# Third attention layer: score products in three single-pass parts instead of one four-pass float32 product

## Chip, cores and metric

One core of one Trainium2 chip runs the whole program. The metric is the device time of one launch in microseconds (us), the median of several runs; lower is better.

## What is computed

Three transformer layers over 512 tokens of width 1024, all in float32: an mLSTM layer (A), a chunked attention layer with relative positions (B), and a third layer (C), each followed by a gated feed-forward part. Only layer C is touched. Cut to what matters:

```python
# differential attention: 4 heads, each with two maps (c = 0, 1) of 64 dimensions
s = einsum('bqhcd,bkhcd->bhcqk', q, k) * d ** -0.5 - slopes * dist
p = softmax(s); a = p[:, :, 0] - lam * p[:, :, 1]; o = a @ v
# neighbourhood attention: 8 heads of 64 dimensions, on a grid 64 wide
s = einsum('bqhd,bikhd->bhqik', q, k) * d ** -0.5 + bias     # a mask of -1e30 outside 16 columns
o = softmax(s) @ v
```

## The kernel before

**Number formats.** Weights and activations of the large products are split into a high part, rounded to the format `F32R`, and a low part, the float32 value less the high one. One large product is then three products of `F32R` parts (helper `three`, L1410 to L1412: high times low, low times high, high times high), each of which TensorE does in one pass. Products on plain float32 tiles are issued as one `matmul`, which the trace shows as two MATMUL records.

**Layer C's attention** is written out by hand for each engine, in a function `attention_c` of its own for ScalarE (L807), VectorE (L1249) and TensorE (L1620), over `C_STEPS` = 32 steps and a few to drain. A step is one tile of 128 queries (`qt`, 0 to 3) of one pair of maps or heads (`n`, 0 to 7): steps 0 to 15 are the four differential heads with their two maps, steps 16 to 31 four pairs of neighbourhood heads. So a pair takes four steps, and a pair changes between steps 3 and 4, 7 and 8, and so on, seven times. In a step `s`

- TensorE makes the scores (L1639): for `a` = 0 and 1 one float32 product of 64 rows (partitions 0 to 63, or 64 to 127) by 128 queries by 512 keys, out of `qk` (queries and keys of the differential heads) or `qkb` (of the neighbourhood heads), into PSUM banks 4 and 5. It then does, in a third each, the "units" of a background stream (`units_of`: the projections of layer C still to come, three `F32R` products of L1410 to L1412 for each k-tile), and between them the transposes of the probabilities of step `s` - 1 (L1670). In the second step of a pair it multiplies the previous pair's probabilities with the values (L1647, L1652), in the third a norm's sum (L1658, differential heads only).
- VectorE takes each score row set out of PSUM with its bias and minimum (L1284), shrinks the slope tile `absd` at the end of a pair (L1288), finishes a head (`yaw`, L1291, in the last step of a pair), evacuates a block of the stream that has ended (`epilogue_of`, L963 or L968), makes the low part of a block of weights (`split_of`, L915), and last turns the exponentials into probabilities (L1311 to L1323).
- ScalarE does the two exponentials (L825), casts (L836, L851), copies the transposes out of PSUM (L844), and makes the high part of the weights (L566).

Each engine takes its instructions strictly in the order written; semaphores connect the engines. `s_done` says that scores are made, `s_biased` that they are out of PSUM, `w_lo` that a block of weights is split.

**The neighbourhood bias** `rpt` (two slots; with 224 KB for a pair of heads in four loads, L412) is loaded from a DRAM scratch by SyncE's queue, among the loads of weights (`load_c_stream`); GpSimd adds the mask to each slot as it lands (L553). Slots 0 and 1 are both loaded at the end of layer B.

**Before step 0** VectorE turns two sums into norm factors in a chain (`both_norms`): reciprocal, two products (L1233, L1235), a copy (L1236), one `split_of` (L915), reciprocal (L1239), product (L1241), on which TensorE waits with the transposes of L1745.

## Time and profile before

| | |
|---|---|
| runs | 2100.31 to 2101.47 us, median 2100.87 us (3 runs) |
| the profiled execution's own time | 2098.9 us |
| its span, first to last instruction | 2097.2 us |
| TensorE busy | 2020.0 us of the span (96%) |
| VectorE, ScalarE, GpSimd busy | 1072.9, 732.7, 37.7 us |
| mean granted TensorE clock | 0.988 of full |
| attention of layer C, step 0 to the last score | 1320.3 to 1546 us of the span |

Times of a row count from the first instruction. A busy time is the union of records, so two products that run side by side count once. "Idle before" is how long an engine stood still ahead of an instruction, with the instruction that released it.

### The profile page before, as it was taken

Reading aid. Unit: us, or ns where it says so; the run is one execution under the profiler, and the core shown is the slowest. Engines: PE = TensorE matmul, PEld = TensorE weight load, DVE = VectorE, ACT = ScalarE, POOL = GpSimd, SP = SyncE. Lnnn points to the kernel's source line nnn. Section 1 sums busy time; section 2 is a strip of 40 time slices with the busy share of each in tenths; the row PEclk is TensorE's granted clock in tenths of the full one; section 3 lists DMA queues with packets and bytes.
Section 4 is the critical chain, followed back from the end, with each engine's and each line's share of the span. In section 5 each row is a group of like instructions: output and inputs, shape, how many; then the busy total and the mean of one; then the engine's idle time right before and its main releaser. Section 6 shows DMA issues by size and latency. Waiting matters only on the chain.

```text
span 2097.2 us, 24349 instructions
## 1 busy us (share of the span) xinstructions
PE 2020.0 (96%) x9435; PEld 1596.2 (76%) x9435; DVE 1072.9 (51%) x1432; ACT 732.7 (35%) x1030; POOL 37.7 (2%) x64
## 2 busy tenths in 40 slices
PE   7999989999999999989999998999999969999998
PEld 5867768888888777668888887766768848888887
DVE  4444565534555444465534557666545565543544
ACT  4444442222233344342222233344433333222222
POOL 1000000000000000000000001000000000000000
PEclk9999999999999999999999999999999989999999
DMA  3211133333324322033333335113222313333322
GB/s 126 81 60 51 41 92 104 86 109 101 93 75 133 101 81 66 31 105 100 85 100 97 92 88 136 60 61 78 58 81 81 100 40 100 95 90 95 100 80 80
DMA packets 297974, 180.15 MB, mean 86 GB/s; under 512 B 22295, under 2 KB 294784, under 8 KB 297896
## 3 DMA queue, kind: packets, MB, share of 16 engines
q1 hardware_dynamic: 297880, 179.08, 29.8%
q8 instruction: 51, 0.84, 0.2%
q14 instruction: 27, 0.22, 0.0%
q10 hardware_dynamic: 16, 0.02, 0.0%
HBM read 176.85 MB, written 2.20 MB: 85 GB/s over the span
## 4 chain that ended last, share of the span: by engine, by line
PE 89%; DVE 6%; ACT 3%; issue 2%; SPq 0%; DMA 0%; DVEq 0%; ACTq 0%
PE psum L1410 27%; PE psum L1412 26%; PE psum L1411 26%; PE psum L1639 2%; DVE wl L915 1%; PE psum L1592 1%; PE psum L1670 1%; PE psum L1601 1%; PE psum L1566 1%; PE psum L1563 1%; PE psum L1614 1%; PE psum L1647 1%; PE psum L1652 1%; ACT wh L566 1%; DVE ss L924 1%
## 5 line engine op out<-in xcount | busy, mean ns | idle before, releaser
L915 DVE TENSOR_TENSOR wl<-stage,wh 128x2048 fp32r<-128x2048 f32 (+3 forms) x182 | 367.6, 2020 | 125.3 <-ACT wh L566 124.5
L566 ACT CAST wh<-stage 128x2048 fp32r<-128x2048 f32 (+3 forms) x182 | 307.1, 1688 | 214.0 <-PE psum L1412 207.4
L1410 PE MATMUL psum<-xl,wh 128*128 128x512 f32 x800 | 327.5, 409 | 11.5 <-DVE xl L930 9.3
L1410 PE MATMUL psum<-x2l,wh 128*128 128x512 f32 x768 | 304.6, 397 | 12.0 <-DVE wl L915 12.0
L1412 PE MATMUL psum<-xh,wh 128*128 128x512 f32 x800 | 313.7, 392 | 0.0
L1411 PE MATMUL psum<-xh,wl 128*128 128x512 f32 x800 | 313.3, 392 | 0.0
L1411 PE MATMUL psum<-x2h,wl 128*128 128x512 f32 x768 | 300.8, 392 | 0.0
L1412 PE MATMUL psum<-x2h,wh 128*128 128x512 f32 x768 | 300.6, 391 | 0.0
L1410 PE MATMUL psum<-hidl,wh 128*128 128x512 f32 x528 | 205.8, 390 | 2.6 <-DVE wl L915 2.6
L1410 PEld LDWEIGHTS psum<-xl,wh 128*128 128x128 f32 x800 | 151.2, 189 | 72.6 <-issue 35.6
L1411 PE MATMUL psum<-hidh,wl 128*128 128x512 f32 x528 | 205.4, 389 | 0.0
L1412 PE MATMUL psum<-hidh,wh 128*128 128x512 f32 x528 | 205.4, 389 | 0.0
L604 ACT ACTIVATE work<-work 128x512 f32<-128x512 f32 x66 | 41.7, 632 | 408.7 <-DVE work L991 408.7
L1410 PEld LDWEIGHTS psum<-x2l,wh 128*128 128x128 f32 x768 | 145.4, 189 | 45.0 <-DVE wl L915 10.1
L1412 PEld LDWEIGHTS psum<-xh,wh 128*128 128x128 f32 x800 | 151.0, 189 | 32.5
L1411 PEld LDWEIGHTS psum<-xh,wl 128*128 128x128 f32 x800 | 151.5, 189 | 30.7 <-issue 2.6
L1412 PEld LDWEIGHTS psum<-x2h,wh 128*128 128x128 f32 x768 | 145.3, 189 | 30.6
L1411 PEld LDWEIGHTS psum<-x2h,wl 128*128 128x128 f32 x768 | 145.4, 189 | 30.3 <-issue 0.7
L991 DVE TENSOR_TENSOR work<-psum,rs 128x512 f32<-128x512 f32 x66 | 45.4, 688 | 211.1 <-PE psum L1412 211.1
L1410 PEld LDWEIGHTS psum<-hidl,wh 128*128 128x128 f32 x528 | 99.1, 188 | 24.2 <-DVE wl L915 3.8
L1410 PE MATMUL psum<-wl,xh 128*128 128x256 f32 x384 | 115.4, 301 | 1.6 <-DVE qk L963 0.8
L1412 PEld LDWEIGHTS psum<-hidh,wh 128*128 128x128 f32 x528 | 99.1, 188 | 20.8
(270 smaller groups left out, 2579.4 us busy)
## 6 DMA issues: line engine op xcount, KB each, us to landing
stage<-in_ffn_w_gate_dram SPq DMA_DIRECT2D x44, 512.0 KB, 4.0
stage<-in_ffn_w_up_dram SPq DMA_DIRECT2D x44, 512.0 KB, 5.3
stage<-in_w_in_dram SPq DMA_DIRECT2D x40, 512.0 KB, 4.0
stage<-in_a_w_in_dram SPq DMA_DIRECT2D x24, 512.0 KB, 4.8
stage<-in_ffn_w_down_dram SPq DMA_DIRECT2D x32, 384.0 KB, 3.8
stage<-in_w_gate_dram SPq DMA_DIRECT2D x22, 512.0 KB, 4.0
stage<-in_w_up_dram SPq DMA_DIRECT2D x22, 512.0 KB, 5.2
stage<-in_ffn_w_down_dram SPq DMA_DIRECT2D x32, 320.0 KB, 3.8
```

Of the source, the lines that this page charges most:

```text
L566: nc.scalar.copy(wh[:, par, 0:n], stage[:, par, 0:n]).then_inc(w_hi, 1)
L604: nc.scalar.activation(work[:, 1, :], work[:, 0, :], ACT.Sigmoid).then_inc(h_sig, 1)
L915: vec.tensor_tensor(wl[:, par, 0:n], stage[:, par, 0:n], wh[:, par, 0:n].bitcast(F32), ALU.subtract).then_inc(w_lo, 1)
L924: vec.tensor_tensor(ss[:, :], ss[:, :], work[:, buf, :], ALU.add).then_inc(ss_added, 1)
L991: vec.tensor_tensor(work[:, 0, :], ps[:, 0, :], rs[:, :], ALU.mult).then_inc(h_in, 1)
L1410: mm(out, a_hi, b_lo, start=start, stop=False)
L1411: mm(out, a_lo, b_hi, start=False, stop=False)
L1412: return mm(out, a_hi, b_hi, start=False, stop=stop)
L1563: mm(psum[:, 6 - 2 * a, t * P:S], av[:, 2 * p + a, t, :], pt[:, a, t, 0:S - t * P], start=(t == 0), stop=(t == TT - 1))
L1566: last = mm(psum[:, 7 - 2 * a, t * P:S], ones[:, :], pt[:, a, t, 0:S - t * P], start=(t == 0), stop=(t == TT - 1))
L1592: mm(psum[:, 4 + a, 0:n], bq[rows, p % 4, qt * P:(qt + 1) * P], bk[rows, p, 0:n], start=True, stop=True).then_inc(s_done, 1)
L1639: mm(psum[:, 4 + a, :], t[rows, n % 4, qt * P:(qt + 1) * P], t[rows, 4 + n % 4, :], start=True, stop=True).then_inc(s_done, 1)
```

## The change

Two tiles are new: `qka` (at 79 KB of the region; it lies over slot 1 of `rpt`) for the differential heads, and `qkn` (at 8 KB, over the keys in `qk`) for the neighbourhood heads. Each holds four tiles of 128 by 512: query high, key high, query low, key low, of one pair at a time. ScalarE makes the two high parts of the next pair (`heads_hi`) in the last step of a pair, after the scores of that step (`s_done`) and after its copies, ahead of its weight cast. VectorE makes the two low parts (`heads_lo`), one as each high part arrives, in the same step after its epilogue and weight split and ahead of the reciprocal. TensorE waits for both low parts (`c_lo`) ahead of the first scores of a pair, and makes three products where it made one, alternating between the two row halves. Slot 1 of `rpt` is first loaded after step 15 instead of before layer C.

```diff
+        qka = at("qka", 79, [P, 4, S], F32R)
+        qkn = at("qkn", 8, [P, 4, S], F32R)
...
             def load_neighbour_bias(p):
 
-                if p < 2:
+                if p == 0:
                     sp.wait_ge(mm_done, st["down11"].b0)
                 else:
                     sp.wait_ge(s_biased, C_SCORE0 + 2 * (DA_STEPS + 4 * (p - 1)))
...
                 load_neighbour_bias(0)
-                load_neighbour_bias(1)
-                p = 2
+                p = 1
...
+            def heads_hi(n):
+
+                t, d = (qk, qka) if n < DA_HEADS else (qkb, qkn)
+                act.wait_ge(block_out, st["C_k" + ("a0", "a1", "b0", "b1")[n // 2]].b0 + 1)
+                if n:
+                    act.wait_ge(s_done, C_SCORE0 + 8 * n)
+                if n == DA_HEADS:
+                    act.wait_ge(c_lo, 2 * DA_HEADS)
+                nc.scalar.copy(d[:, 0, :], t[:, n % 4, :]).then_inc(c_hi, 1)
+                nc.scalar.copy(d[:, 1, :], t[:, 4 + n % 4, :]).then_inc(c_hi, 1)
...
+                    if part == 3 and s + 1 < C_STEPS:
+                        heads_hi(n + 1)
                     for b in c_stream.splits(s):
                         split_of(b)
...
+            def heads_lo(n):
+                t, d = (qk, qka) if n < DA_HEADS else (qkb, qkn)
+                for i in range(2):
+                    dve.wait_ge(c_hi, 2 * n + i + 1)
+                    vec.tensor_tensor(d[:, 2 + i, :], t[:, 4 * i + n % 4, :], d[:, i, :].bitcast(F32),
+                                      ALU.subtract).then_inc(c_lo, 1)
...
                     for b in c_stream.splits(s - 1):
                         split_of(b)
+                    if qt == TT - 1 and s + 1 < C_STEPS:
+                        heads_lo(n + 1)
...
-                        if qt == 0 and n % 2 == 0:
-                            pe.wait_ge(block_out, st["C_k" + ("a0", "a1", "b0", "b1")[n // 2]].b0 + 1)
+                        if qt == 0:
+                            pe.wait_ge(c_lo, 2 * (n + 1))
                         if s:
                             pe.wait_ge(s_biased, C_SCORE0 + 2 * s)
-                        t = qk if s < DA_STEPS else qkb
-                        for a in range(2):
-                            rows = slice(DH * a, DH * a + DH)
-                            mm(psum[:, 4 + a, :], t[rows, n % 4, qt * P:(qt + 1) * P], t[rows, 4 + n % 4, :],
-                               start=True, stop=True).then_inc(s_done, 1)
+                        d = qka if s < DA_STEPS else qkn
+                        for part, (i, j) in enumerate(((0, 3), (2, 1), (0, 1))):
+                            for a in range(2):
+                                rows = slice(DH * a, DH * a + DH)
+                                last = mm(psum[:, 4 + a, :], d[rows, i, qt * P:(qt + 1) * P], d[rows, j, :],
+                                          start=(part == 0), stop=(part == 2))
+                                if part == 2:
+                                    last.then_inc(s_done, 1)
```

The first pair's parts are made ahead of step 0 (`heads_hi(0)` after the table load L816, `heads_lo(0)` ahead of the work on `absd`).

VectorE's queue in step 7, the last of the second pair, before (L1284 scores out of PSUM, L1288 `absd`, L1291 `yaw`, L1311 to L1319 the probabilities):

```order
L1284 ISA work,rowmax<-psum,absd 128x512 [waits t_done,s_done]
L1284 ISA rowmax 128x1
L1288 TENSOR_SCALAR absd<-absd 128x896 [waits s_biased]
L1291 SCALAR_TENSOR_TENSOR yaw<-psum,gains,ss 128x512 [waits d_rs]
L1311 RECIPROCAL rowinv<-rowsum 128x2 [waits s_exp]
```

and as changed (line numbers of the changed kernel):

```order
L1308 ISA work,rowmax<-psum,absd 128x512 [waits t_done,s_done]
L1308 ISA rowmax 128x1
L1312 TENSOR_SCALAR absd<-absd 128x896 [waits s_biased]
L1315 SCALAR_TENSOR_TENSOR yaw<-psum,gains,ss 128x512 [waits d_rs]
L1269 TENSOR_TENSOR qka<-qk,qka 128x512 [waits c_hi] x2
L1337 RECIPROCAL rowinv<-rowsum 128x2 [waits s_exp]
```

Two subtractions, each with a wait for ScalarE, have come in ahead of the reciprocal; in steps 3, 11, 19 and 27 an epilogue and a weight split stand between the scores and these two.

ScalarE's queue in the same step, as changed (L839 exponentials, L850 the cast of `yah`, L858 the copy of the transposes, L568 the weight cast):

```order
L839 ACTIVATE work,rowsum<-work,rowmax 128x512 [waits s_biased] x2
L850 CAST yah<-yaw 128x512 [waits d_full]
L858 COPY pt<-psum 128x4x128 [waits t_done]
L817 CAST qka<-qk 128x512 [waits s_done,block_out]
L818 CAST qka<-qk 128x512
L568 CAST wh<-stage 128x2048 [waits mm_done,w_loaded1]
```

The two casts of L817 and L818 are new, between the copy and the weight cast.

SyncE's queue at the end of layer B, where the bias loads stand among those of the weights, before

```order
L412 DMA rpt<-rp_scratch 64x14x64 [waits mm_done]
L412 DMA rpt<-rp_scratch 64x14x64 x3
L412 DMA rpt<-rp_scratch 64x14x64 [waits mm_done]
L412 DMA rpt<-rp_scratch 64x14x64 x3
L400 DMA stage<-in_w_in_dram 128x4x256 [waits w_lo]
```

and as changed

```order
L403 DMA stage<-in_w_in_dram 128x4x256
L415 DMA rpt<-rp_scratch 64x14x64 [waits mm_done]
L415 DMA rpt<-rp_scratch 64x14x64 x3
L403 DMA stage<-in_w_in_dram 128x4x256 [waits w_lo]
```

Four of the eight loads have left this place; they come back after nine more blocks of weights, with a wait for `s_biased` of step 15.

## Rows read from the trace of the kernel before

**Rows 1.** Page, part 4: the chain that ended last, by engine.

```profile
PE 89%; DVE 6%; ACT 3%; issue 2%; SPq 0%; DMA 0%; DVEq 0%; ACTq 0%
```

**Rows 2.** Timeline, TensorE, step 4's scores: start us, us, engine, line, operation.

```profile
1342.80 0.39 PE L1412 MATMUL psum<-xh,wh 128*128 128x512 f32 x1
1343.12 1.13 PE L1639 MATMUL psum<-qk 64*128 64x512 f32 x4
1344.18 0.50 PE L1410 MATMUL psum<-xl,wh 128*128 128x512 f32 x1
1344.52 0.39 PE L1411 MATMUL psum<-xh,wl 128*128 128x512 f32 x1
1344.74 0.40 PE L1412 MATMUL psum<-xh,wh 128*128 128x512 f32 x1
```

**Rows 3.** Lines L1639 and L1658, TensorE: ns min/median/max, first and last start.

```profile
L1639 PE MATMUL psum<-qk x64: 589/641/693, 1320.3 to 1424.3; 64*128 64x512 f32 x64
L1658 PE MATMUL psum<-ss,ones x8: 592/644/697, 1359.4 to 1446.9; 128*128 128x512 f32 x8
```

**Rows 4.** Timeline, weight loads of step 4's scores.

```profile
1343.12 0.30 PEld L1639 LDWEIGHTS psum<-qk 64*128 64x128 f32 x4 [0.35 <-issue]
```

**Rows 5.** Timeline, VectorE: reciprocals of steps 3, 11 and 19, step 11's split.

```profile
1343.77 0.16 DVE L1311 RECIPROCAL rowinv<-rowsum 128x2 f32<-128x2 f32 x1
1399.54 2.28 DVE L915 TENSOR_TENSOR wl<-stage,wh 128x2048 fp32r<-128x2048 f32 x1
1401.74 0.16 DVE L1311 RECIPROCAL rowinv<-rowsum 128x2 f32<-128x2 f32 x1
1459.63 0.16 DVE L1311 RECIPROCAL rowinv<-rowsum 128x2 f32<-128x2 f32 x1
```

**Rows 6.** Timeline, TensorE: first scores of five pairs; a wait in step 12.

```profile
1371.99 1.13 PE L1639 MATMUL psum<-qk 64*128 64x512 f32 x4
1400.43 1.13 PE L1639 MATMUL psum<-qk 64*128 64x512 f32 x4
1403.39 0.66 PE L1670 MATMUL psum<-ident,work 128*128 128x128 f32 x4 [0.25 <-DVE work L1319]
1459.74 1.13 PE L1639 MATMUL psum<-qkb 64*128 64x512 f32 x4
1488.87 1.13 PE L1639 MATMUL psum<-qkb 64*128 64x512 f32 x4
```

**Rows 7.** Groups by line: operations like the added ones and the copy; count, busy, mean ns.

```profile
L606 ACT CAST hidh<-work 128x512 fp32r<-128x512 f32 x24 | 14.9, 621 | 35.6 <-DVE work L996 35.6
L998 DVE TENSOR_TENSOR hidl<-work,hidh 128x512 fp32r<-128x512 f32 x24 | 16.6, 693 | 16.5 <-ACT hidh L606 16.5
L1317 DVE TENSOR_SCALAR work<-work,rowinv 128x512 f32<-128x512 f32 x16 | 7.6, 478 | 0.0
```

**Rows 8.** Timeline, ScalarE: the last copies of steps 7 and 23.

```profile
1370.44 0.58 ACT L844 COPY pt<-psum 128x512 f32<-128x512 f32 x1
...
1487.55 0.59 ACT L844 COPY pt<-psum 128x512 f32<-128x512 f32 x1 [1.22 <-PE psum L1670]
```

**Rows 9.** Timeline before step 0: VectorE, GpSimd, ScalarE, TensorE.

```profile
1294.28 4.30 DVE L1236 COPY ss<-rs 128x512 f32<-128x512 f32 x1
1298.50 2.28 DVE L915 TENSOR_TENSOR wl<-stage,wh 128x2048 fp32r<-128x2048 f32 x1
...
1293.84 4.44 POOL L553 TENSOR_TENSOR rpt<-rpt,namask 128x1792 f32<-128x1792 f32 x1 [1.42 <-DMA rpt<-rp_scratch]
...
1295.02 1.89 ACT L566 CAST wh<-stage 128x2048 fp32r<-128x2048 f32 x1
...
1304.82 0.59 PE L1745 MATMUL psum<-ident,rs 8*128 8x8 f32 x4 [5.10 <-DVE rs L1241]
```

**Rows 10.** A wait of TensorE in layer A, and the clock (eighth column) after it.

```profile
273.61 0.50 PE L1410 MATMUL psum<-ygl,wh 128*128 128x512 f32 x1 [2.61 <-DVE wl L915]
...
274.00:277.40 3.40, 3.40 (x10) 2.63 (x9) 2.61 (x4) 2.68 (x5) 0.00 (x0) 0.50 0.70 202
```

More of the change, by code:

```diff
@@ L311, in build @@
         t_done, t_out, pv_done, y_hi, y_lo = (sem(n) for n in ("t_done", "t_out", "pv_done", "y_hi", "y_lo"))
+        c_hi, c_lo = sem("c_hi"), sem("c_lo")
         d_sq, d_ss, d_ln, d_rs, d_full, absd_ready, absd_scaled = (
@@ L816, in attention_c @@
                 nc.scalar.preload_act_table_set(LN_EXP)
+                heads_hi(0)
                 for b in c_stream.splits(-1):
@@ L1255, in attention_c @@
                 split_of(first + 3)
+                heads_lo(0)
                 dve.wait_ge(absd_ready, 1)
```

## The prediction

> **What bounds the kernel now.** The page comes first: TensorE is busy 96% of the span, and the chain of waits that ends last lies on TensorE for 89% of the time [rows 1]. So a microsecond taken from TensorE's queue in layer C counts, and so does each one that TensorE has to wait. The second view is TensorE's timeline around one pair of score products. Ordinary single-pass products start 0.22 to 0.23 us apart. The four records of the scores' two float32 products start at 1343.12, and from the L1412 ahead of them (1342.80) to the second product behind them (L1411, 1344.52) go 1.72 us [rows 2]. Two ordinary distances (0.46) would be there anyway, so a step's scores cost TensorE 1.26 us, and 32 steps cost 40.3 us. The third view is where VectorE and ScalarE stand when a pair ends, since that is where the change puts its new work [rows 5, 6, 8]. The fourth is the norm chain before step 0, where TensorE stands idle for 5.10 us [rows 9]: whatever the moved bias load does there counts too.
>
> **Scores on TensorE.** The two row halves run side by side now: the scores' four records take 1.13 us together, and their shortest and longest records (589 and 693 ns) are those of the sum in L1658 (592 and 697), which uses all 128 rows [rows 2, 3]. In each case one record takes 0.10 more than the other. The row halves' second pair of records starts 1.13 - 0.59 = 0.54 after the first, and 0.10 of it I read as weights that could not be loaded ahead of the switch. A float32 record then takes 0.44, and a product of two records four times a single pass (0.23). At the other end the next L1410 starts at 1344.18, 0.07 before the scores' end at 1344.25, and it too lasts 0.10 longer than the 0.40 of the ordinary one [rows 2]: the switch drains what is under way and then shows one weight load.
>
> The three new passes, with the halves side by side and the switches as now: the first starts at 0, the second at 0.10 + 0.23, the third at 0.56, which ends 0.39 later at 0.95 instead of 1.13. The product behind starts 0.18 sooner. So the gain is 0.18 a step, **5.8 us** in 32 steps, and not the quarter that the pass count suggests. Bounds: if no switch cost anything, three passes are 0.69 against 1.26, a gain of 0.57 a step or 18.2 us; if the halves ran one after the other there would be three more distances of 0.23, a loss of 0.51 a step or 16.3 us. I take 0.18, since switches of this kind are what the rows show on both sides of the scores.
>
> The Trainium skill bears on this. TensorEngine Tiling (Array Packing), section Overview, Key Properties, says that a change of tiling mode, unlike a change of tile, drains TensorE. By it the 0.18 stands; without a drain the gain would be the upper bound above.
>
> **Waits of TensorE for the new parts.** ScalarE's casts are worth 0.62 each and VectorE's subtractions 0.69 each [rows 7], 16 of each. The first two of each lie in the wait for block C_va0's products, before step 0, and cost nothing; if that cover were gone they would cost about 2.5 us. The other fourteen stand in the last step of a pair, and TensorE waits for them ahead of the next scores. An instruction starts about 0.08 before the end of the one ahead on VectorE (L915 to L1311 [rows 5]); for ScalarE I take 0.10.
>
> In steps 3, 11 and 19 the subtractions start where the reciprocal started, and the second ends 0.61 + 0.69 later; with 0.05 to be noticed that is 1.35 after the reciprocal's old start. Step 3: 1343.77 + 1.35 = 1345.12, where the scores started at 1343.12 [rows 2, 5]: 2.00. Step 11: 1401.74 + 1.35 = 1403.09 against 1400.43: 2.66. Step 19: 1459.63 + 1.35 = 1460.98 against 1459.74: 1.24 [rows 5, 6]. In steps 7 and 23 ScalarE's casts come last, behind its copy of the transposes: 0.48 + 0.62 to the first high part, 0.03 to be noticed, 0.61 + 0.69 for the two subtractions and 0.05, in all 2.48 after the copy's start. Step 7: 1370.44 + 2.48 = 1372.92 against 1371.99: 0.93. Step 23: 1487.55 + 2.48 = 1490.03 against 1488.87: 1.16 [rows 6, 8]. Steps 15 and 27 read in the same way leave about 0.5 each. Both sides of these differences move 0.18 earlier with the shorter scores, so they stand. The sum is 9.0. Off it go the 0.25 us that TensorE waits today in step 12 for step 11's probabilities [rows 6], which the late scores cover: **8.7 us**. Behind the subtractions wait the reciprocal and the probabilities (1.6 us, from 1401.74 to 1403.34 in step 11, where TensorE's transposes waited [rows 6]); the transposes come 2.5 after the scores, so with scores as late as the subtractions that is covered by 0.8, and the cost there is nothing. The weight cast behind ScalarE's new casts is wanted two blocks later; that delay costs nothing either.
>
> **Clock.** A wait of TensorE of 2.61 us in layer A was followed by 3.4 us at half the clock [rows 10]. Step 11's wait is as long as that one. Half of 3.4 is lost: **1.7 us**. The bounds are 0, and 3.4 if step 3's wait of 2.0 does the same, of which the trace has no example.
>
> **The moved bias load.** GpSimd's second addition of the mask (1293.84, for 4.44) lies exactly beside VectorE's copy L1236, which takes 4.30 for 512 columns and ends when the addition does [rows 9]; that copy should cost about 0.5, as the scaling L1317 of as many columns does (478 ns [rows 7]). With slot 1 loaded later the addition goes away from there. VectorE's next instruction, the split L915, then no longer follows at 1298.50 but as soon as ScalarE's cast is done, 1295.02 + 1.89 = 1296.91. That is 1.5 us sooner, and TensorE's idle time of 5.10 behind it becomes 3.6: **1.5 us** gained. The bounds are 0 and 3.8 (the copy's full excess). The addition comes back after step 15, with the load behind a wait on SyncE's queue; the weights queued behind it are only wanted at step 16's split, and there it may hold back VectorE's scaling of the probabilities for some 4 us, in the step ahead of the one in which TensorE has the value products before the transposes. I count it as nothing; without that cover it would cost up to 4.
>
> **Sum.** -5.8 + 8.7 + 1.7 - 1.5 = **+3.1 us**. The profiled execution took 2098.9, 2.0 less than the median of 2100.87. Against its own time that is 2102.0; against the median **2103.9 us**. Differences within 0.2% (4.2 us) I call no change: about what a measurement of this kernel can tell from none.
>
> **Rivals.**
> *The switch is cheaper for single-pass products.* The 0.10 on either side may belong to the float32 records as such. With only the start delay (0.09) and the next product's 0.11, three passes cost 0.89 and the gain is 0.37 a step, 11.8 us; the sum becomes -2.9, and if step 11's wait leaves the clock alone as well, -4.6. For it: nothing shows a single-pass product in row halves. Against: the 0.10 also stands on the ordinary L1410 behind the scores. Chance 0.2, half of it beyond 0.2%.
> *The waits do not come.* The casts and subtractions would have to be done before TensorE arrives, and the change would then do what it says at no price: -7.3 us. Against it is the order of the queues, which puts them behind a split of 2.28 us. Chance 0.08.
> *Weights of the second and third pass are loaded in the open.* Then each pass after the first costs the 0.10 that the first pays, 0.20 a step, 6.4 us, and the result is +9.5, slower. It decides once loads of one row half wait for that half's product. Against it: the scores' four loads are over within 0.30 us, while the first records still run for 0.4 [rows 2, 4]. For it: the second two of them belong to the same float32 product. Chance 0.13.
> The Trainium skill, TensorE: Matmul & The Clock Gate, Part 3, The mechanism, has this as a rule: a weight load overlaps a running product only when the row group differs. The four loads above do not agree.
> *The halves run one after the other* (single-pass alone, since the float32 ones do not): +25, slower. Chance 0.05.
> *More stretches at half the clock*, behind the waits of 1 to 2 us, at 1.7 each, or the mask's addition in a place without cover: +5 to +8, slower. Chance 0.1.
>
> **How the numbers follow.** My forecast has 0.44; its own range is +0.5 to +5, nearly all of it no change. Faster: 0.1 from the first rival, 0.08 from the second and a little of the forecast's tail, **0.2**. Slower: 0.13 + 0.05 + 0.1, **0.28**. No change: **0.52**. The range reaches down to -6.9 and up to the third rival: **2094.0 to 2111.0**; the serial case and half of the case without waits stay outside.
>
> **What would show it.** In the changed profile the scores' six records should span 0.95 us and the product behind start 0.88 after the first; 0.7 would mean free switches, 1.15 open weight loads, 1.6 halves in turn. TensorE should show idle time ahead of the first scores of seven pairs, released by VectorE's subtraction in L1269, some 8.7 us in all and the longest ahead of step 12, with a granted clock of half behind it. L1236's copy should take 0.5 and TensorE's idle time ahead of the norm's transposes 3.6. If the seven waits come to under 5 us or over 12, the reading of the queues is wrong; if the scores gain over 0.35 a step, the reading of the switch is.

## Result and profile after

| | before | changed |
|---|---|---|
| median of the runs | 2100.09 us (20 runs) | 2107.36 us (20 runs) |
| profiled execution, its span | 2098.9, 2097.2 us | 2107.4, 2105.6 us |
| first scores of layer C (start in the span) | 1320.25 | 1318.40 |
| first to last scores of layer C | 224.7 us | 231.9 us |
| last scores of layer C to the end of the span | 552.2 us | 555.3 us |
| mean granted TensorE clock | 0.988 | 0.985 |

The changed kernel takes 1.003 times the time of before (95% interval 1.0023 to 1.0036): 0.3% slower, 7.3 us. The three stretches of the table add up to the difference of the spans: -1.85 + 7.2 + 3.1 = 8.4. The first two are where the change works; the third lies behind the attention of layer C, where nothing was changed. The first also moves without any change: a second trace of the kernel before has its first scores at 1322.66 and a span of 2099.5 us, so against that one the spans differ by 6.1 us and not by 8.4. The 7.3 between the medians lie between the two.

In what follows `x_scores` and the like are names of experiments. Line numbers are those of each kernel; in the changed one the stream's products are L1436 to L1438, the scores L1666, the transposes of the probabilities L1699, the parts L817, L818 and L1269, the weight cast L568 and the split L931.

**The scores.** Timeline of TensorE of the changed kernel around the scores of step 2, and its weight loads (start, us, engine, line, operation), against [rows 2, 4]:

```profile
1328.97 0.39 PE L1438 MATMUL psum<-xh,wh 128*128 128x512 f32 x1
1329.29 0.96 PE L1666 MATMUL psum<-qka 64*128 64x512 f32 x6
1330.19 0.50 PE L1436 MATMUL psum<-xl,wh 128*128 128x512 f32 x1
...
1329.29 0.53 PEld L1666 LDWEIGHTS psum<-qka 64*128 64x128 f32 x6 [0.35 <-issue]
```

Six records span 0.96 where four spanned 1.13, and the product behind starts 0.90 after the first (before 1.06). It still lasts 0.50 instead of 0.40. The six weight loads are over after 0.53, while products run.

**The waits for the parts.** The first scores of the seven later pairs, with TensorE's idle time ahead of them in brackets, against [rows 6]:

```profile
1342.64 1.30 PE L1666 MATMUL psum<-qka 64*128 64x512 f32 x6 [1.92 <-DVE qka L1269]
1373.33 0.96 PE L1666 MATMUL psum<-qka 64*128 64x512 f32 x6 [0.86 <-DVE qka L1269]
1403.80 1.05 PE L1666 MATMUL psum<-qka 64*128 64x512 f32 x6 [2.56 <-DVE qka L1269]
1433.92 0.96 PE L1666 MATMUL psum<-qkn 64*128 64x512 f32 x6 [0.34 <-DVE qkn L1269]
1465.16 0.97 PE L1666 MATMUL psum<-qkn 64*128 64x512 f32 x6 [1.17 <-DVE qkn L1269]
1494.82 0.96 PE L1666 MATMUL psum<-qkn 64*128 64x512 f32 x6 [1.09 <-DVE qkn L1269]
1526.26 0.96 PE L1666 MATMUL psum<-qkn 64*128 64x512 f32 x6 [0.45 <-DVE qkn L1269]
```

They sum to 8.4 us. VectorE's queue in step 11, ahead of the longest (compare [rows 5], where the reciprocal came at 1401.74 right behind the split):

```profile
1400.26 2.28 DVE L931 TENSOR_TENSOR wl<-stage,wh 128x2048 fp32r<-128x2048 f32 x1
1402.45 1.29 DVE L1269 TENSOR_TENSOR qka<-qk,qka 128x512 fp32r<-128x512 f32 x2
1403.66 0.16 DVE L1337 RECIPROCAL rowinv<-rowsum 128x2 f32<-128x2 f32 x1
```

**The clock.** Busy time of each engine, and in the eighth column the granted clock, behind the waits of 1.92 and 2.56 and between them, against [rows 10]:

```profile
1343.10:1346.50 3.40, 3.40 (x12) 2.15 (x9) 2.39 (x7) 1.52 (x4) 0.00 (x0) 0.50 0.82 282
1346.50:1404.50 58.00, 53.30 (x287) 38.96 (x285) 35.59 (x75) 27.35 (x51) 0.00 (x0) 1.00 0.13 40
1404.50:1407.90 3.40, 3.40 (x12) 2.44 (x9) 2.99 (x9) 1.52 (x4) 0.00 (x0) 0.51 0.77 264
```

Before, nothing from 1320 to 1545 ran at 1.2 GHz. Now two stretches of 3.4 us do. The same view of the kernel before:

```profile
1320.00:1545.00 225.00, 222.27 (x1116) 152.55 (x1114) 135.18 (x271) 103.87 (x200) 8.55 (x2) 1.00 0.23 65
```

**Before step 0**, against [rows 9]:

```profile
1294.60 0.42 DVE L1252 COPY ss<-rs 128x512 f32<-128x512 f32 x1
1297.27 2.29 DVE L931 TENSOR_TENSOR wl<-stage,wh 128x2048 fp32r<-128x2048 f32 x1 [2.25 <-ACT wh L568]
...
1303.61 0.59 PE L1774 MATMUL psum<-ident,rs 8*128 8x8 f32 x4 [3.56 <-DVE rs L1257]
```

The copy takes 0.42 instead of 4.30, the split behind it now waits for ScalarE's cast, and TensorE stands idle for 3.56 instead of 5.10.

**Where the mask addition went.** GpSimd's addition for slot 1 now lies beside VectorE's work of step 16. GpSimd and VectorE, then TensorE in step 17, where it transposes the probabilities of step 16:

```profile
1437.94 4.02 POOL L555 TENSOR_TENSOR rpt<-rpt,namask 128x1792 f32<-128x1792 f32 x1 [144.71 <-DMA rpt<-rp_scratch]
...
1438.25 5.87 DVE L931 TENSOR_TENSOR wl<-stage,wh 128x2048 fp32r<-128x2048 f32 x1
1444.04 0.15 DVE L1337 RECIPROCAL rowinv<-rowsum 128x2 f32<-128x2 f32 x1
...
1447.89 0.63 PE L1699 MATMUL psum<-ident,work 128*128 128x128 f32 x4 [0.44 <-ACT pt L858]
```

The split takes 5.87 instead of 2.29, the probabilities behind it come that much later, ScalarE's copy of their transposes then stands behind the next exponentials, and TensorE waits 0.44 for it. On TensorE the cost shows in step 17.

**The end of the program.** The last norm's sums (L1813, before L1784) and the 32 transposes behind them. The first fence is of the kernel before, the second of the changed kernel, and the third shows the busy times and the clock (eighth column) of the changed one there:

```profile
2086.97 1.06 PE L1784 MATMUL psum<-ones,ss 128*128 128x8 f32 x8 [2.17 <-DVE ss L924]
2087.89 3.69 PE L1722 MATMUL psum<-ident,post 128*128 128x128 f32 x32
```

```profile
2093.61 1.53 PE L1813 MATMUL psum<-ones,ss 128*128 128x8 f32 x8 [2.17 <-DVE ss L940]
2095.00 6.54 PE L1751 MATMUL psum<-ident,post 128*128 128x128 f32 x32
```

```profile
2094.00:2100.80 6.80, 6.80 (x35) 6.80 (x35) 4.51 (x7) 0.29 (x1) 0.00 (x0) 0.50 0.26 106
```

Both kernels have the same wait of 2.17 us there. Before, the clock stayed at 2.4 GHz behind it; after, it was 1.2 GHz for 6.8 us, and the transposes took 6.54 instead of 3.69. From this wait's end to the end of the span it takes 12.0 us instead of 10.2, so 1.8 of the 3.1 us lie here; before, VectorE's work on the transposed tiles (5.36 us from its first to its last instruction) took longer than the transposes, and that hides the rest of what these lost. The other 1.3 us lie further ahead. TensorE has waits of 3.53, 7.61 and 4.7 us behind layer C's attention in both kernels, with 1.2 GHz around them, but not at the same moments of the work: the longest such stretch began 0.8 us after the end of the first wait before (1697.34) and 0.3 us ahead of it as changed (1701.50). Between the first two of these waits the changed kernel needs 0.7 us more, between the third and the one of 2.17 another 0.7, and 0.2 came off ahead of them.

### The profile page after: what moved, and what is told of

Its sections match the earlier page's. It is cut to its first block, busy times and chain, and to the rows that moved or that the text cites. A ratio compares the mean times of both kernels' runs of the same rounds, so it can differ in the third digit from the quotient of the medians.

```text
span 2105.6 us, 24520 instructions
## 1 busy us (share of the span) xinstructions
PE 2022.3 (96%) x9499; PEld 1607.4 (76%) x9499; DVE 1079.1 (51%) x1448; ACT 741.3 (35%) x1046; POOL 37.0 (2%) x64
## 4 chain that ended last, share of the span: by engine, by line
PE 87%; DVE 7%; ACT 4%; issue 2%; SPq 0%; DMA 0%; DVEq 0%; ACTq 0%
PE psum L1436 26%; PE psum L1437 25%; PE psum L1438 25%; DVE wl L931 2%; PE psum L1666 1%; PE psum L1618 1%; PE psum L1699 1%; PE psum L1627 1%; PE psum L1592 1%; PE psum L1589 1%; PE psum L1640 1%; ACT wh L568 1%; PE psum L1681 1%; DVE ss L940 1%; PE psum L1552 1%
## 5 line engine op out<-in xcount | busy, mean ns | idle before, releaser
L931 DVE TENSOR_TENSOR wl<-stage,wh 128x2048 fp32r<-128x2048 f32 (+3 forms) x182 | 374.8, 2060 | 128.3 <-ACT wh L568 127.5
L568 ACT CAST wh<-stage 128x2048 fp32r<-128x2048 f32 (+3 forms) x182 | 307.2, 1688 | 209.0 <-PE psum L1438 202.2
L1436 PE MATMUL psum<-xl,wh 128*128 128x512 f32 x800 | 328.7, 411 | 12.4 <-DVE xl L946 9.9
L1438 PE MATMUL psum<-xh,wh 128*128 128x512 f32 x800 | 314.5, 393 | 0.0
L1436 PE MATMUL psum<-x2l,wh 128*128 128x512 f32 x768 | 305.1, 397 | 8.8 <-DVE wl L931 8.8
L1438 PE MATMUL psum<-x2h,wh 128*128 128x512 f32 x768 | 301.0, 392 | 0.0
L1436 PE MATMUL psum<-hidl,wh 128*128 128x512 f32 x528 | 205.8, 390 | 2.6 <-DVE wl L931 2.6
L1438 PE MATMUL psum<-hidh,wh 128*128 128x512 f32 x528 | 205.4, 389 | 0.0
L1436 PEld LDWEIGHTS psum<-xl,wh 128*128 128x128 f32 x800 | 151.7, 190 | 68.5 <-issue 29.6
L1436 PEld LDWEIGHTS psum<-x2l,wh 128*128 128x128 f32 x768 | 145.5, 190 | 42.2 <-DVE wl L931 7.0
L1438 PEld LDWEIGHTS psum<-xh,wh 128*128 128x128 f32 x800 | 151.6, 189 | 32.9
L1438 PEld LDWEIGHTS psum<-x2h,wh 128*128 128x128 f32 x768 | 145.6, 190 | 30.9
L1436 PEld LDWEIGHTS psum<-hidl,wh 128*128 128x128 f32 x528 | 99.1, 188 | 24.5 <-DVE wl L931 3.8
L1436 PE MATMUL psum<-wl,xh 128*128 128x256 f32 x384 | 115.1, 300 | 1.6 <-DVE qk L979 0.8
L1438 PEld LDWEIGHTS psum<-hidh,wh 128*128 128x128 f32 x528 | 99.1, 188 | 20.8
```

The lines of the kernel that those rows point to most:

```text
L568: nc.scalar.copy(wh[:, par, 0:n], stage[:, par, 0:n]).then_inc(w_hi, 1)
L931: vec.tensor_tensor(wl[:, par, 0:n], stage[:, par, 0:n], wh[:, par, 0:n].bitcast(F32), ALU.subtract).then_inc(w_lo, 1)
L1436: mm(out, a_hi, b_lo, start=start, stop=False)
L1438: return mm(out, a_hi, b_hi, start=False, stop=stop)
```

## Experiments

Medians stand beside a median of before from the same chip and batch: 2100.37 for the first four experiments, 2099.48 for the next four, 2100.44 for the last three. "C" is the time from the first to the last scores of layer C in the profiled execution. It is the sharper measure of what happens there, since the stretches before and behind it move by 1 to 3 us with the clock. All thirteen traces (both kernels, a second trace of each, nine experiments) are compared in this way.

### Only the bias load moved

The kernel before, with slot 1 loaded after step 15 as the change does:

```diff
-                if p < 2:
+                if p == 0:
                     sp.wait_ge(mm_done, st["down11"].b0)
...
                 load_neighbour_bias(0)
-                load_neighbour_bias(1)
-                p = 2
+                p = 1
```

> The kernel before with one piece of the change: slot 1 of the neighbourhood bias is loaded after step 15 instead of before layer C. Theory 1 (the early addition of the mask holds VectorE's copy, and the copy holds the norm chain): the copy falls from 4.30 to 0.42 us, step 0 starts 1.2 to 1.9 us sooner, and the time is about 1.5 us below the kernel before, ratio 0.9993. Rival (the copy hides behind ScalarE's cast, or the addition costs as much where it comes back): the time is that of the kernel before within 0.5 us.

Measured: 2101.09, ratio 1.0002 [0.9993, 1.0011]; C 224.88. The copy and the idle time are as in the changed kernel:

```profile
1295.36 0.42 DVE L1235 COPY ss<-rs 128x512 f32<-128x512 f32 x1
...
1304.37 0.41 PE L1744 MATMUL psum<-ident,rs 8*128 8x8 f32 x4 [3.56 <-DVE rs L1240]
```

So the local gain of 1.54 is real (the first scores start at 1318.89, 1.36 sooner than before), and the total did not show it: a miss. The last row of this kernel's TensorE says where the larger part went. Behind the same wait of 2.17 its final transposes ran at half the clock:

```profile
2088.75 6.40 PE L1721 MATMUL psum<-ident,post 128*128 128x128 f32 x32
```

From the last scores to the end it took 555.5 us, 3.3 more than before, 1.8 of it behind this wait. Step 17 takes 9.92 us here, against 9.73 before and 10.20 in the changed kernel: here the split began just ahead of the addition and took its 2.28, and the scaling behind it was held back instead, as the prediction expected.

### Only the scores

The changed kernel, with parts made for pairs 0 and 4 alone (`n + 1 == DA_HEADS` as the condition of both `heads_hi` and `heads_lo`, and waits to match). It leaves out the parts of the other six pairs: their scores are computed from those of pair 0 or 4, with the same number and shape of products.

> The changed kernel without the parts of pairs 1 to 3 and 5 to 7: the high and low parts are made for pair 0 and pair 4 only, and the scores of the other pairs are computed from those, so this part of the computation is left out. TensorE waits for parts once, ahead of step 16. Theory 1 (the three single-pass products save 0.17 us a step, and the waits of the other six pairs are what made the change slow): 5.6 from the scores and 1.9 from the bias load, less 0.3 for the one wait left, so 7.2 us below the kernel before, ratio 0.9966, no half clock between 1312 and 1690. Rival (the new products slow something beside themselves, or the waits only took the place of others that come back): less than 3 us below the kernel before.

Measured: 2094.69, ratio 0.9971 [0.9961, 0.9982]; C 220.8, that is 3.9 less than before. TensorE's waits in layer C, grouped by releaser (us in total, times, longest):

```profile
PE psum L1701 <- ACT ss L845: 1.9, 3, 0.7
PE psum L1701 <- DVE work L1349: 0.6, 1, 0.6
PE psum L1701 <- ACT pt L858: 0.4, 1, 0.4
PE psum L1701 <- DVE work L1345: 0.4, 1, 0.4
PE psum L1668 <- DVE qkn L1269: 0.3, 1, 0.3
```

It was expected 7.2 below the kernel before and came out 5.7 below. The waits left are those of the kernel before but for two, and no stretch of layer C's attention is at half the clock. Ahead of it next to nothing was gained, where 1.9 was expected: the first scores start at 1319.97, with 6.8 us at half the clock in front of them. An ordinary step takes 5.67 instead of 5.83, so 31 steps gain some 5.1. Of that 0.4 goes to the one wait for parts that is left (step 15 to 16), about 0.6 to step 17 with the mask addition (10.14 instead of the 9.56 that it takes in `x_best`), and 0.2 to step 12, which stays at 6.30: with nothing late ahead of it, its wait for probabilities grows to 0.4.

### Only the parts

The changed kernel with the old products; the parts are made and waited for, and not used:

```diff
-                        d = qka if s < DA_STEPS else qkn
-                        for part, (i, j) in enumerate(((0, 3), (2, 1), (0, 1))):
...
+                        t = qk if s < DA_STEPS else qkb
+                        for a in range(2):
+                            rows = slice(DH * a, DH * a + DH)
+                            mm(psum[:, 4 + a, :], t[rows, n % 4, qt * P:(qt + 1) * P], t[rows, 4 + n % 4, :],
+                               start=True, stop=True).then_inc(s_done, 1)
```

> The changed kernel with the four-pass float32 scores of before: the parts are made and waited for, but not used. Theory 1: the waits stay at 8.4 us in all with the longest ahead of steps 4 and 12 (1.9 and 2.6), the clock is at half behind these two (3.4 us), and 1.9 come off for the bias load, so 10 us above the kernel before, ratio 1.0047; 5.6 us above the changed kernel on the same chip less what differs between runs. Rival (the waits only bite since the scores are shorter): waits under 5 us, and a time under 4 us above the kernel before.

Measured: 2109.93, ratio 1.0048 [1.0034, 1.0061]; C 235.0, 10.3 more than before and 3.1 more than the changed kernel, which gains 5.1 by its products and loses 1.5 by a second stretch at half the clock and 0.4 in step 17. Both the time (10 above before was expected) and the waits came as expected, the stretch behind step 3's wait did not. The waits, and the clock behind those of 1.92 and 2.58:

```profile
PE psum L1665 <- DVE qka L1269: 5.4, 3, 2.6
PE psum L1665 <- DVE qkn L1269: 3.0, 4, 1.1
```

```profile
1343.00:1346.50 3.50, 3.49 (x17) 2.34 (x18) 2.61 (x8) 1.39 (x4) 0.00 (x0) 1.00 0.87 291
1404.40:1407.70 3.30, 3.30 (x9) 1.73 (x6) 2.86 (x7) 1.19 (x3) 0.00 (x0) 0.50 0.87 296
```

The waits are the same 8.4 with the old products: they come from the parts alone. The first of the long waits, of the same length as in the changed kernel, leaves the clock at full speed here. That of 2.55 to 2.58 was followed by half the clock in each of the four traces that have it.

### The other order in a pair's last step

`heads_hi` right behind the exponentials on ScalarE; on VectorE the low parts, then the probabilities, then epilogue and split (`blocks_of_step`):

```diff
-                    for b in c_stream.splits(s - 1):
-                        split_of(b)
-                    if qt == TT - 1 and s + 1 < C_STEPS:
+                    late = qt == TT - 1 and s + 1 < C_STEPS
...
+                    if late:
                         heads_lo(n + 1)
+                    else:
+                        blocks_of_step()
...
+                    if late:
+                        blocks_of_step()
```

> The changed kernel with another order in the last step of a pair: ScalarE makes the high parts right behind the exponentials, ahead of its other casts and copies, and VectorE makes the low parts and then the probabilities ahead of the epilogue and the weight split. Theory 1 (the seven waits come from what stands ahead of the parts in the two queues): the waits fall from 8.4 us to under 0.5 and the half clock behind steps 4 and 12 goes, so about 7.5 us below the kernel before, ratio 0.9964. Rival (the work is too much for the step wherever it stands, and the epilogue or the weight split is now late for the stream's products): TensorE waits for w_lo or block_out instead, and the time stays above the kernel before.

Measured: 2096.75, ratio 0.9982 [0.9973, 0.9991]; C 224.0. All waits for parts are gone and no stretch of layer C's attention is at half the clock, yet of the 11.5 us that waits and clock had cost in the changed kernel only 7.9 came back, and the time is 3.6 below before where 7.5 was expected. The new waits are for ScalarE's copies of the transposes, which now stand behind the casts; neither the expectation nor its rival had them:

```profile
PE psum L1707 <- ACT pt L860: 2.9, 6, 1.0
...
PE psum L1684 <- ACT pt L860: 0.8, 2, 0.4
```

### A second buffer for the parts

Parts of two pairs at once, in space over both bias slots and over `qk`; they are made in the second or third step of the pair before, behind the copies and the probabilities. Both bias slots are loaded inside layer C:

```diff
-        qka = at("qka", 79, [P, 4, S], F32R)
-        qkn = at("qkn", 8, [P, 4, S], F32R)
+        qkp = [at(f"qkp{i}", kb, [P, 4, S], F32R) for i, kb in enumerate((72, 80, 8, 0, 16))]
+        parts_of = (0, 1, 0, 1, 2, 3, 4, 2)
...
-                    if part == 3 and s + 1 < C_STEPS:
-                        heads_hi(n + 1)
+                    if part == 1 + n % 2 and n + 1 < C_STEPS // TT:
+                        heads_hi(n + 1)
...
+                    if qt == 1 + n % 2 and n + 1 < C_STEPS // TT:
+                        heads_lo(n + 1)
```

> The changed kernel with a second buffer for the parts: pairs 0 to 3 alternate between 72 and 80 KB of the region, pairs 4 to 7 take 8, 0, 16 and 8 KB. The parts of the next pair are made one or two steps earlier, in the second or third step of a pair, behind all other work of that step; both slots of the bias are loaded inside layer C, after steps 11 and 15. Theory 1 (the waits come from making the parts in the last step, behind its epilogue and split, and the half clock comes from the waits): no wait of TensorE for the parts, no half clock from step 0 to the end of layer C's attention, 5.3 us less from first to last scores than the kernel before (224.7 there) or a little more, and 6 to 8 us below it in all, ratio 0.9968. Rival (the 16 casts and 16 subtractions cost on ScalarE and VectorE wherever they stand): new waits of 3 us or more for copies, probabilities or splits, and less than 3 us below the kernel before.

Measured: 2096.26, ratio 0.9984 [0.9975, 0.9993]; C 221.4, 3.3 less than before where 5.3 was expected, and the time 3.2 below before where 6 to 8 was. No wait for parts, and no half clock in layer C's attention. One wait of 1.1 is new, and GpSimd's mask addition is behind it:

```profile
1431.11 5.01 POOL L551 TENSOR_TENSOR rpt<-rpt,namask 128x1792 f32<-128x1792 f32 x1 [25.39 <-DMA rpt<-rp_scratch]
...
1430.00 2.29 DVE L927 TENSOR_TENSOR wl<-stage,wh 128x2048 fp32r<-128x2048 f32 x1
1432.20 0.16 DVE L1331 RECIPROCAL rowinv<-rowsum 128x2 f32<-128x2 f32 x1
1432.40 4.40 DVE L1343 TENSOR_SCALAR work<-work,rowinv 128x512 f32<-128x512 f32 x2
```

The two scalings take 0.88 elsewhere.

### Stream products ahead of a pair's first scores

The changed kernel with the first third of the step's stream in front of the scores where a pair begins:

```diff
+                    ahead = qt == 0 and 0 < s < C_STEPS
+                    if ahead:
+                        units_of(c_stream, s, 0, 3)
...
-                    units_of(c_stream, s, 0, 3)
+                    if not ahead:
+                        units_of(c_stream, s, 0, 3)
```

> The changed kernel with TensorE doing the first third of the background stream ahead of the scores in the first step of a pair, so that it has 1.4 us of work before it needs the parts; the rest of the order stays. If the half clock behind the waits is real and theirs: waits ahead of scores and of the transposes behind them fall from 8.4 to about 3.5 us, none over 1.3, and the two stretches at half clock (1.7 each) go as well, so about 8 us below the changed kernel. Rival (clock stretches come anyway, for reasons of their own): only the 5 us of waits.

Measured: 2101.34, ratio 1.0004 [0.9995, 1.0013], against before; 5.5 below the changed kernel in the same batch, where 8 was expected, and 5 by the rival. C 226.6. TensorE's waits there, and the clock of the whole stretch:

```profile
PE psum L1703 <- ACT pt L858: 3.9, 4, 1.0
...
PE psum L1669 <- DVE qka L1269: 1.8, 2, 1.2
PE psum L1703 <- DVE work L1345: 1.1, 2, 0.5
```

```profile
1320.00:1546.00 226.00, 216.73 (x1173) 157.02 (x1169) 141.85 (x285) 110.72 (x214) 12.35 (x3) 1.00 0.27 69
```

Of the 8.4 for parts, 1.8 is left and the clock is whole, so the time does not tell the expectation from its rival, but the clock's column does. Scores that come later make everything behind them late: 3.9 for the copies.

### One half's three products, then the other's

```diff
-                        for part, (i, j) in enumerate(((0, 3), (2, 1), (0, 1))):
-                            for a in range(2):
+                        for a in range(2):
+                            for part, (i, j) in enumerate(((0, 3), (2, 1), (0, 1))):
```

> The changed kernel with the three score products of one row half issued one after the other and then those of the other half, instead of taking turns. If the halves run side by side whatever the order, the six records span 0.96 us as now and the time is the changed kernel's. If a product only runs beside its direct neighbour in the queue, only the third and fourth overlap: five distances of 0.23 instead of two, 1.5 to 1.65 us a step, and 17 to 22 us above the changed kernel.

Measured: 2108.13, ratio 1.0039 [1.0025, 1.0053], C 231.8: within layer C's attention as the changed kernel (232.0 in this batch, 2106.85 in all; the difference lies ahead of step 0, where the first scores start 2.2 us later).

```profile
1330.98 0.97 PE L1666 MATMUL psum<-qka 64*128 64x512 f32 x6
1331.87 0.50 PE L1436 MATMUL psum<-xl,wh 128*128 128x512 f32 x1
```

The row halves run side by side in this order too.

### The changed kernel once more

> The changed kernel once more, for a second trace. The seven waits come from the order of the queues and should return within 0.05 us each (8.4 in all). The stretches at half clock behind them should come again behind the wait of 2.6; behind that of 1.9 either way. What the trace showed beyond layer C (3 us more than the kernel before, with other stretches at half clock near the end) should differ from trace to trace if it is chance, and come again if it is the change's.

Measured: 2106.85, ratio 1.0035 [1.0021, 1.0048], C 232.0, waits of 1.91, 0.86, 2.56, 0.34, 1.17, 1.09 and 0.45, two stretches of 3.4 at half the clock, 555.2 us behind the last scores. All of it repeats. Not every loss of clock does: one of the changed kernel's 20 runs took 2102.23 us at a mean clock of 0.988, the others 2105.75 to 2108.88 at 0.982 to 0.987.

### The second buffer, with VectorE's queue put in order

`x_double`, with the low parts made one step later, while ScalarE does the exponentials, and every weight split of steps 1 to 31 put behind the probabilities:

```diff
+                    if qt == 2 + n % 2 and n + 1 < C_STEPS // TT:
+                        heads_lo(n + 1)
...
-                    for b in c_stream.splits(s - 1):
-                        split_of(b)
+                    if s == 0 or s >= C_STEPS:
+                        for b in c_stream.splits(s - 1):
+                            split_of(b)
...
+                    if 0 < s < C_STEPS:
+                        for b in c_stream.splits(s - 1):
+                            split_of(b)
```

> The kernel with two buffers for the parts, and two moves in VectorE's queue besides: the low parts are made while the exponentials run, in the step behind ScalarE's high parts, and the weight split of a step stands behind its probabilities instead of ahead of them. Theory 1 (what is left of the scores' gain goes to TensorE's waits of 0.4 to 1.1 us for probabilities and copies): from first to last scores 219.5 to 220.5 us against 224.7 in the kernel before, no wait for parts, none for step 11's probabilities, and 1.0 to 1.5 us below the two-buffer kernel, so 4.5 to 5 below the kernel before, ratio 0.9978. Rival (the split is now late for the stream): waits of TensorE on the split, and a time at or above the two-buffer kernel's.

Measured: 2095.74, ratio 0.9977 [0.9968, 0.9986], C 219.3. Of TensorE's waits one group is left; the last three rows are the kernel before's own, for comparison:

```profile
PE psum L1699 <- ACT ss L841: 2.5, 4, 0.7
```

```profile
PE psum L1670 <- ACT ss L831: 1.9, 3, 0.7
PE psum L1670 <- DVE work L1323: 0.6, 1, 0.6
PE psum L1670 <- DVE work L1319: 0.2, 1, 0.2
```

It beats both kernels: 4.7 us below before, as expected, and some 11 below the changed kernel.

### Its control, and before once more

`x_control` is the kernel before with all of `x_best` but the parts: its float32 scores, both slots loaded late, the splits behind the probabilities.

> The kernel before, with its float32 scores, but with both slots of the bias loaded inside layer C and the weight split behind the probabilities, as in the best kernel. It tells what the three-part scores themselves are worth in a good order. Theory 1 (0.17 us a step): the best kernel lies 4.5 to 5.5 us below this one, and this one 1 us below the kernel before or level with it. Rival (what was gained came from the queues' order alone): the two lie within 2 us of each other.

Measured: 2100.06, ratio 0.9995 [0.9986, 1.0004], C 224.7. So the 4.3 us between it and `x_best`, just under the 4.5 to 5.5 expected, come with the three-part scores. Both have half the clock at the end (555.5 and 554.9 us behind the last scores). In C they differ by 5.4. Of that some 0.5 is the mask addition, which holds step 16's scalings back in `x_control` (step 17 takes 10.19) and comes too late for that in `x_best` (9.56); the other 4.9 are 0.16 a step.

> The kernel before once more, for a second trace. The stretches at half clock behind the attention of layer C (from the last scores to the end 552.2 us in the first trace, 552 to 555.5 in those of the other kernels): if they fall by chance, this trace may show 555 as well as 552; if the end of the program at full clock belongs to this kernel, it shows 552 again.

Measured: 2100.16, ratio 1.0002 [0.9993, 1.0011], C 224.7 and 552.1 us behind it, both as in the first trace. What differs lies ahead: the first scores start 2.4 us later. The wait of [rows 10], on which the prediction's price for the clock rests, stands in this trace too, and the clock behind it (eighth column) stayed whole:

```profile
274.88 0.50 PE L1410 MATMUL psum<-ygl,wh 128*128 128x512 f32 x1 [2.61 <-DVE wl L915]
...
275.00:279.50 4.50, 2.90 (x12) 2.06 (x12) 3.71 (x6) 2.89 (x5) 0.00 (x0) 1.00 0.78 215
```

A wait of 2.08 us near 118.5 did the opposite: full clock behind it in the first trace, 3.4 us at half in the second. So one and the same kernel goes either way at the same wait.

## Where the prediction was right and where it was wrong, step by step

The range held the time, thanks to its width: it reached 10 us up for a rival that did not come. The likeliest case, no change, did not come either: 7.3 us slower where 3.1 were forecast and 4.2 was the bound. The mechanisms named are the ones that the traces show. Two terms were mis-sized, the clock and the mask addition, and one was missing, the clock behind the attention.

**Scores, right.** Forecast 0.18 a step. Measured 0.16 to 0.17: ordinary steps go from 5.83 to 5.67, others from 6.00 to 5.84, 7.91 to 7.75 or 6.43 to 6.26, some 5.1 over 31 steps. (`x_best` shows 5.4 less than before, 0.5 of it from step 12's old wait.) The reading of the switch (a late start and an exposed weight load on either side) holds, and with it the rule of the Trainium skill (TensorEngine Tiling (Array Packing), Tiling Modes, Key Properties; the prediction names the wrong section) that a change of mode drains TensorE: both sides still show the 0.10.

**Waits for the parts, right.** Forecast 2.00, 0.93, 2.66, 0.5, 1.24, 1.16 and 0.5; measured 1.92, 0.86, 2.56, 0.34, 1.17, 1.09 and 0.45. Each makes its step 0.06 longer than its row says (step 11 takes 8.32 instead of 5.70), 8.85 in all. Off it goes 0.45, step 12's old wait and what came with it, for which I had 0.25: 8.4 against the forecast 8.7. `x_parts` has them without the new products, `x_scores` the new products without six of them.

**Clock inside layer C, mis-sized.** I charged one stretch at half the clock, 1.7. There were two, behind the waits of 2.56 and 1.92; steps 12 and 4 take 7.20 and 7.21 where `x_best` takes 5.67 and 5.69, and the waits are in the steps ahead: 1.5 each, 3.05 in all. The prediction held the second as a bound "of which the trace has no example". In fact that trace had two of nearly that length, 2.08 near 118.6 us and 2.17 at the end of the program, and the clock stayed whole behind both; only other traces show half the clock behind them. Nor was the price for step 11's wait as firm as one row made it. The wait of 2.61 in layer A is in all thirteen traces: in six the clock fell within 1.5 us behind it, in seven it stayed whole until a further wait of 2.1 us. In layer C's attention it did fall behind step 11's wait, in all four traces that have it, so the term came out; the row that it was taken from left that open.

**The moved bias load, half right.** TensorE's idle time fell to 3.56 as worked out, 1.54 gained. "I count it as nothing", said of the mask addition's new place, was wrong by about 0.6 (0.5 against before, whose step had the dearer scores): step 17 takes 10.20, against 9.73 before and 9.56 in `x_best`. I expected VectorE's scaling of the probabilities to be held back, as it was in `x_bias`; in the changed kernel it was the split ahead of it, for 3.6 us. What the 1.5 gained is worth in the whole is less sure: the first scores start at 1317.9 to 1320.3 in the eleven traces with the moved load, at 1320.3 and 1322.7 in the two without, as stretches at half the clock fall ahead of them. The Trainium skill (SBUF — State Buffer, section SBUF: two separate sides) calls the port that GpSimd and VectorE share an exclusive lock, taken by a VectorE operation with two SBUF inputs as well. The rows agree: the split, with its two inputs, took 5.87 beside the addition of 4.02 that had begun before it. In `x_double` the split began first, at its usual 2.29, and the addition lasted 5.01 instead of 4.02.

**Behind the attention, missing.** I took all behind layer C's attention as unchanged. It costs 3.1 more, 1.8 of it behind the wait of 2.17 at the end and 1.3 around the three longer waits ahead of that. The wait of 2.17 stands there in all thirteen traces. In four (both of before, `x_scores`, `x_order`) the transposes behind it run at 2.4 GHz, in the other nine, among them `x_bias` and `x_control` with C as before, they start at 1.2 GHz. From the last scores to the end the four take 552.1 to 552.3, the nine 554.4 to 555.5. The length of the wait does not decide it, and neither do the new scores, which `x_scores` and `x_order` have too. What also differs between the kernels is when the wait comes, since everything ahead was shortened or lengthened; that this decides is a guess, and the cause stays open. Each of the two kernels repeated its own case in its second trace. It hit `x_bias` and `x_control`, which leave the scores alone, and `x_best` pays for it too.

**The sum** with the measured terms: in layer C -5.1 + 8.4 + 3.05 + 0.6 = 7.0 against 7.2 measured, ahead of it -1.5, behind it +3.1. That makes 8.6, against 8.4 between the two profiled spans and 7.3 between the medians. Without the second stretch in layer C's attention (1.5) and the loss behind it (3.1) it would have been 4.0, still inside what I called no change.

**Rivals.** Cheaper switches: refuted, 0.16 to 0.17 a step. Waits that do not come: refuted. Weights loaded in the open: refuted; six loads in 0.53 us beside running products, and 0.90 to the product behind. That rule of the Trainium skill (TensorE: Matmul & The Clock Gate, Part 3, The mechanism: loads overlap products only of another row group) does not agree with these rows, nor with the ordinary products, whose loads of all 128 rows are hidden at 0.23 a product; the same section also lets a load into a background buffer be pulled ahead, and with that the rows agree. Halves in turn: refuted, in both orders of issue. More stretches at half the clock and an uncovered mask addition, at 0.1: this is what came, in part, with the one at the end of the program on top.

## What to carry to other kernels

The arithmetic was right and its placement was not: a cheaper product on the bound engine paid 5.1 us and cost 8.4 in waits and 3 in clock because its operands were made in the last step before their use, behind other work in both helping engines' queues. With a second buffer the same work is done earlier, where TensorE does not wait for it, and the same products give 4.3 us. Price a wait of some 2 us or more on TensorE at its length, and give a chance, not a certainty, to half of each stretch at the lower clock behind it: look in more than one trace for every wait of that length and what followed. And ask of a moved GpSimd operation which VectorE instruction will stand beside it.

## What was not expected of the hardware

- The same wait at the same place in the program (2.17 us) was followed by full clock in four traces and by half in nine, with 3.69 or 4.98 to 6.61 us for the same 32 transposes. The wait of 2.08 near 118 us was followed by half the clock in eight of thirteen traces, that of 2.61 in layer A in six of thirteen, within 1.5 us, that of 1.9 in layer C in three of four, that of 2.55 to 2.58 there in four of four; none of up to 1.2 us in layer C's attention was. The kernel before alone shows both cases at 2.08 and at 2.61.
- Products of two row halves run side by side even when one half's three are issued before the other's first: 0.97 us for the six, against 0.96 in turn.
- GpSimd's addition holds up more than copies: a split for 3.6 us, two scalings for 3.5 (4.40 against 0.88), a copy for 3.9. A reciprocal of 128 by 2 in `x_double` did not wait (0.16), nor did one of 128 by 512 in the kernel before that began 1.2 us into an earlier addition (3.35).
